# A hybrid decoder layer on one core: an adding load, a fifth weight slot and an earlier block product

## The chip, the core and the metric

One core of a Trainium2 chip runs the whole layer in one launch. TensorE (PE) multiplies, VectorE (DVE) and ScalarE (ACT) prepare its operands and take its results, GpSimd (POOL) does small work and issues some DMAs, SyncE (SP) issues most DMAs. The engines have a queue each, run it in order, and meet at semaphores. The metric is device time in microseconds from the first to the last instruction and what lies around them, lower is better.

## What is computed

```python
def reference(x, ...):
    h = rmsnorm(x, norm_pre_mix)
    proj = h @ w_in                          # 512 x 1024 by 1024 x 4168
    y_a = hgrn2_mixer(...)                   # gated linear recurrence
    y_b = dsa_mixer(...)                     # indexer, top 128 keys, attention
    x = x + rmsnorm(concat(y_a, y_b) @ w_o, norm_post_mix)
    h = rmsnorm(x, norm_pre_ffn)
    ff = silu(h @ w_gate) * (h @ w_up)       # hidden size 2816
    ff = ff @ w_down
    return x + rmsnorm(ff, norm_post_ffn)
```

Sequence 512, model width 1024, float32. The change touches the feed-forward part alone (the two lines that make `ff`, and the norm behind them).

## The kernel before

**Arithmetic.** Every weight matrix stays float32 in value: an operand is split into a high part, rounded to the type that the matmul takes, made by ACT, and a low part, the rest, made by DVE as operand minus high part. Each product is then three matmuls, low times high, high times low, high times high.

**Gate and up.** The first four chunks of 256 columns of the gate and up weights (`J_FF` to `J_FF + 3`) go through `feature_group` (L1638), 24 matmuls for each half `m` of a chunk. The other 18 (`NS`) go through a scheme that computes a 2 x 2 block product from seven smaller products: `block_product(n, i)` (L1978), 12 matmuls of 256 columns each. Product 1 of block `n` is passed on by ACT (`pass_on(n, 0)`, L960) to the bank in which product 6 accumulates, so product 6 waits for that copy. DVE makes the weight sums (`block_sums`, L1457 to L1461) and takes the results (`cut`, `take`, L1480 to L1495).

**Down.** `w_down` has 22 row tiles, in 11 pairs. They run in 21 steps `d` (`STEPS`): ten steps of kind "one" (pairs 0 to 9, the first sweep), one step "all" (pair 10, step `MID` = 10), ten steps "two" (pairs 0 to 9 again, the second sweep). A step "one" is four products of 6 matmuls of 512 columns (`step_product`, L2016), a step "two" three. Before a step, this happens:
- SP loads its weights into a raw slot (L599 to L604): for "one" two transfers, the whole first row tile (512 KB, columns 0 to 1023 of the slot) and the right half of the second row tile (256 KB, columns 1024 to 1535). There are four slots, `WL[d % 4]`, so the load of step `d` waits until PE has done step `d - 4`.
- DVE makes sums in place (`step_sums`, L1511 to L1513 for "one"). With the slot's four quarters q0 to q3: q2 = q2 + q1, then q1 = q0 + q1, then q3 = q2 + q0. For "two" two smaller sums (L1516, L1517).
- ACT sets one quarter aside for the second sweep (L971), makes the high parts of the weights (L979, `columns_of_step_hi`) and of the activations (L991 to L998).
- DVE makes the low parts of the weights (L1522, `columns_of_step_lo`) and of the activations (L1530 to L1536, `rows_of_step_lo`).

DVE's order in the first sweep is, for each `d`: `rows_of_step_lo(d)`, `step_sums(d + 1)`, `columns_of_step_lo(d)`. So the low weights of step `d` stand behind the arrival of the weights of step `d + 1`. In the second sweep it is `step_sums(d + 1)`, `columns_of_step_lo(d)`, `rows_of_step_lo(d)`. At the seam between block products and first sweep DVE runs `step_sums(1)`, `columns_of_step_lo(0)`, `take(16)`, and PE's step 0 waits for all three (`s_dlo`, `s_free`). PE runs steps 18, 19 and 20 in an interleaved order at the end: 18 matmuls of steps 18 and 19, then step 20 is wanted.

POOL issues, after the 36th block result (`s_gu2`), the load of the last gain, then waits for the end of the first sweep and reloads `x2`.

Of the kernel before, what the change touches and what calls it, by code (L numbers as in the profile page):

```python
# [7 lines left out]
P = 128  # L8
# [26 lines left out]
def hymba_layer(nc, x, w_in, lb_logits, hgrn_gnorm, rel_bias, w_o, norm_pre_mix, norm_post_mix,  # L35
# [3 lines left out]
    TB = S // P  # L39
# [70 lines left out]
    with ExitStack() as ctx:  # L110
# [3 lines left out]
        def sem(name):  # L114
            return ctx.enter_context(nc.semaphore(name))
# [53 lines left out]
        def a1(o, n):  # L169
            return A1[:, o:o + n]  # L170
# [44 lines left out]
        T_RAW = {1: a1(20480, 1024), 2: a1(21504, 1024), 3: a1(2048, 1024), 4: A2[:, 6912:7936]}  # L215
        RING = (0, 1, 4)
        SUMS = (3, 2)
        squares, fin = hT_f[:, 0:4 * D], hT_f[:, 4 * D:8 * D].rearrange("p (t n) -> p t n", t=TB)
        first_sum, third_sum = hT_f[:, 6144:7168], hT_f[:, 7168:8192]
        junk = a1(18432, 1024)  # L220
        junk_mid = a1(10240, 1024)
# [228 lines left out]

        WL = (0, 3, 2, 4)

        def step_raw(d):
            return W_f[:, WL[d % 4], :]

        def step_lo(d):
            return W_r[:, WL[d % 4], :]

        def step_hi(d):
            return (s_w[:, 0:CH], W_r[:, 1, :], s_t[:, 0:2, :].rearrange("p i n -> p (i n)"))[d % 3]  # L460
# [23 lines left out]
            return t.rearrange("p (k n) -> p k n", n=256)  # L484

        def down_landed(eng, d):
            eng.wait_ge(s_dw[d % 4], sum(32 if STEPS[e][0] == "one" else 16 for e in range(d % 4, d + 1, 4)))

        def steps_done(eng, n):
            if n == NB:  # L490
                eng.wait_ge(s_acc, 4)
            else:
                eng.wait_ge(s_step, n - (n > NB))
# [67 lines left out]
        @block.sync  # L561
        def _(sp):
            for t in range(TB):
                if t == 2:
                    sp.dma_start(raw_view(0)[:, 0:4, :], raw_src(0)[:, 0:4, :]).then_inc(s_raw_half, 16)
                sp.dma_start(xin[:, t, :], x_d[t * P:(t + 1) * P, :]).then_inc(s_x[t], 16)
            sp.dma_start(raw_view(0)[:, 4:8, :], raw_src(0)[:, 4:8, :]).then_inc(s_raw[0], 16)
            sp.dma_start(lbt[:, :, :], lb_logits.rearrange("r (h p) -> p r h", p=P)).then_inc(s_small, 16)
            sp.dma_start(gn[:, :], hgrn_gnorm.rearrange("a p -> p a")).then_inc(s_small, 16)
            sp.dma_start(tab, rel_bias).then_inc(s_small, 16)  # L570
            sp.dma_start(oh_sb, onehot).then_inc(s_small, 16)
            sp.dma_start(far[:, :], rel_bias[N_BUCKETS - 1, :].partition_broadcast(P)).then_inc(s_far, 16)
            for j in range(1, J_FF + 4):
                if j == J_IKW:
                    sp.dma_start(raw_view(j), raw_src(j)).then_inc(s_ikw, 16)
                    continue
                if ring_of(j) >= 2:
                    sp.wait_ge(s_lo, j - 2 if j - 2 <= J_IKW else j - 1)
                sp.dma_start(raw_view(j), raw_src(j)).then_inc(s_raw[ring_of(j) % 2], 16)
            for n, j in enumerate(range(J_FF + 4, J_DN)):  # L580
                if n < 2:
                    sp.wait_ge(s_lo, j - 1)
                elif n == 2:
                    sp.wait_ge(s_gu, 8)
                else:
                    sp.wait_ge(s_gu2, 2 * (n - 2))
                sp.dma_start(view(ring3(n), j), raw_src(j)).then_inc(s_raw3[n % 3], 16)
            for d, (kind, c) in enumerate(STEPS):
                if d == 0:
                    sp.wait_ge(s_gu2, 2 * (NS - 2))  # L590
                elif d < 3:
                    sp.wait_ge(s_prod, 3 * (NS - 2 + d))
                elif d == 3:
                    sp.wait_ge(s_gu2, 2 * NS)
                else:
                    steps_done(sp, d - 3)
                x, y = [wd[(2 * c + k) * P:(2 * c + k + 1) * P, :] for k in range(2)]
                if kind == "one":
                    sp.dma_start(step_raw(d)[:, 0:D], x).then_inc(s_dw[d % 4], 16)  # L599
                    sp.dma_start(step_raw(d)[:, D:D + 512], y[:, 512:D]).then_inc(s_dw[d % 4], 16)  # L600
                elif kind == "two":
                    sp.dma_start(step_raw(d)[:, 0:D], y).then_inc(s_dw[d % 4], 16)
                else:
                    sp.dma_start(view(step_raw(d), J_DN + c), raw_src(J_DN + c)).then_inc(s_dw[d % 4], 16)  # L604
            for i, t in enumerate(LAST):
                for half in range(2):
                    c = slice(half * 512, (half + 1) * 512)
                    sp.wait_ge(s_fin, 2 * i + half + 1)
                    sp.dma_start(out_d[t * P:(t + 1) * P, c], x2[:, t, c]).then_inc(s_out, 16)
            sp.wait_ge(s_out, 16 * 2 * TB)  # L610
# [3 lines left out]
        def _(pool):  # L614
# [99 lines left out]
                inv_of(8 + k)  # L714
            pool.wait_ge(s_x2, TB)
            pool.dma_start(x2_d, A2[:, 0:TB * D]).then_inc(s_x2s, 16)
            pool.wait_ge(s_gu2, 2 * NS)
            pool.dma_start(gain_out, norm_post_ffn[0, :].partition_broadcast(P)).then_inc(s_go, 16)
            pool.wait_ge(s_x2s, 16)
            steps_done(pool, NB)  # L720
# [365 lines left out]
        def _(dve):  # L1086
            n_chain = [0]

            def link(ins):
                n_chain[0] += 1  # L1090
                ins.then_inc(s_dve, 1)
                dve.wait_ge(s_dve, n_chain[0])
# [413 lines left out]
            def step_sums(d):  # L1506
                kind, c = STEPS[d]
                down_landed(dve, d)
                q = step_raw(d).rearrange("p (q n) -> p q n", q=4)
                if kind == "one":  # L1510
                    link(dve.tensor_tensor(q[:, 2], q[:, 2], q[:, 1], ALU.add))  # L1511
                    dve.tensor_tensor(q[:, 1], q[:, 0], q[:, 1], ALU.add)  # L1512
                    dve.tensor_tensor(q[:, 3], q[:, 2], q[:, 0], ALU.add).then_inc(s_dsum, 1)  # L1513
                else:
                    p = pair_raw(c)
                    dve.tensor_tensor(pieces(q[:, 2]), kept(c), pieces(q[:, 0]), ALU.add)  # L1516
                    dve.tensor_tensor(p[:, 1], p[:, 1], p[:, 2], ALU.add).then_inc(s_dsum, 1)  # L1517
# [117 lines left out]
        def _(pe):  # L1635
# [314 lines left out]
            GATE_UP_BANKS = {J_FF: (0, 1), J_FF + 1: (2, 3), J_FF + 2: S_BANKS[0][1:], J_FF + 3: S_BANKS[1][1:]}  # L1950
            for j in range(J_FF, J_FF + 4):
                pe.wait_ge(s_lo, j + 1)
                for m in range(2):
                    if j == J_FF + 2:
                        pe.wait_ge(s_t4, 3)
                    elif j == J_FF + 3:
                        pe.wait_ge(s_fr, m + 1)
                    feature_group(w_split(j), m, P, GATE_UP_BANKS[j][m], S // 2 if j < J_FF + 2 else 0, S, s_gu)

            def block_product(n, i, fresh=False):  # L1960
                y, z, f = S_BANKS[n % 2]
                out = {1: PS[:, y, 0:256], 2: PS[:, y, 0:256], 3: PS[:, z, 0:256], 4: PS[:, f, 0:256],
# [16 lines left out]
                                      stop=(k == 3 and p == 2), skip_group_check=True)  # L1979
                return o  # L1980

            pe.wait_ge(s_tlo, 3)
            for n in range(NS):
                pe.wait_ge(s_wl[0], n + 1)
                if n >= 2 and n % 2 == 0:
                    pe.wait_ge(s_free, n // 2)
                elif n >= 2:
                    pe.wait_ge(s_fr, n + 2)
                block_product(n, 1, True).then_inc(s_prod, 1)
# [123 lines left out]
```

## Time and profile before

| what | us |
|---|---|
| median of 3 runs (lowest, highest) | 667.36 (665.61, 667.52) |
| the profiled execution | 664.93 |
| its span, first to last instruction | 663.2 |
| PE busy in the span | 651.1 |
| DVE busy | 548.3 |
| ACT busy | 350.3 |
| POOL busy | 92.2 |
| first down sweep, first matmul of step 0 to that of step 10 | 543.91 to 603.36 |
| second down sweep, first matmul of step 11 to the last matmul | 614.24 to 657.01 |

The profile is of one execution, which was 2.4 us faster than the median of the timed runs. Times inside it are from the start of the span. PE is nearly always busy, so the first thing to look for is where it is not, and then who ends each of those gaps.

### The profile page before, as it was taken

How to read it: one execution, taken by the hardware profiler on the slowest of the kernel's cores; microseconds unless marked ns; L12 is line 12 of the kernel's file. 1: busy time of each engine (PE TensorE's matmuls, PEld its weight loads, DVE VectorE, ACT ScalarE, POOL GpSimd, SP SyncE). 2: the span in 40 equal slices, each digit the busy share in tenths (PEclk: the TensorE clock that was granted, in tenths of full speed). 3: DMA queues.
4: the chain of work that ended last, by engine and by line, in shares of the span. 5: the costliest groups of instructions: out<-in, count | busy, mean ns of one | idle time of the engine just before them, and what ended most of it. 6: DMA issues, size and time to landing. Idle time of an engine off the chain costs nothing.

```text
span 663.2 us, 10196 instructions
## 1 busy us (share of the span) xinstructions
PE 651.1 (98%) x4017; PEld 580.3 (88%) x4017; DVE 548.3 (83%) x769; ACT 350.3 (53%) x564; POOL 92.2 (14%) x131
## 2 busy tenths in 40 slices
PE   8999999999999999999999999999999999999986
PEld 6878888888888889888998999999999998778875
DVE  6766999998988768345886988989989979998787
ACT  6656433443349577235643555555554565663563
POOL 4800220000405378002100000000000000000001
PEclk9999999999999999999999999999999999999998
DMA  8453042352521301252332423324324235444423
GB/s 277 129 162 113 13 127 65 99 174 77 190 65 64 126 2 36 92 191 64 118 137 63 127 65 127 110 84 127 96 96 128 86 114 183 142 143 191 127 95 128
DMA packets 51266, 75.53 MB, mean 114 GB/s; under 512 B 5393, under 2 KB 40209, under 8 KB 50962
## 3 DMA queue, kind: packets, MB, share of 16 engines
q1 hardware_dynamic: 47360, 62.78, 29.8%
q0 software_dynamic: 3568, 11.55, 4.7%
q8 instruction: 32, 0.52, 0.3%
q10 hardware_dynamic: 290, 0.55, 0.2%
q14 instruction: 16, 0.13, 0.1%
HBM read 70.12 MB, written 6.84 MB: 116 GB/s over the span
## 4 chain that ended last, share of the span: by engine, by line
PE 86%; DVE 10%; ACT 2%; DMA 1%; issue 1%; POOL 0%; DVEq 0%; ACTq 0%; POOLq 0%
PE PS L1638 38%; PE PS L1978 27%; PE PS L2016 7%; PE PS L1857 2%; DVE W_r L1522 2%; PE PS L1712 2%; PE PS L2027 2%; PE PS L1688 1%; PE PS L1687 1%; PE PS L1868 1%; PE PS L1791 1%; PE PS L1682 1%; DVE W_f L1512 1%; DVE A L1630 1%; DVE W_f L1511 1%
## 5 line engine op out<-in xcount | busy, mean ns | idle before, releaser
L1638 PE MATMUL PS<-hT_lo,w_hi 128*128 128x512 f32 (+2 forms) x280 | 102.0, 364 | 0.0
L1638 PE MATMUL PS<-hT_hi,w_hi 128*128 128x512 f32 (+2 forms) x280 | 100.7, 360 | 0.0
L1638 PE MATMUL PS<-hT_hi,w_lo 128*128 128x512 f32 (+2 forms) x280 | 100.7, 359 | 0.0
L1097 DVE TENSOR_TENSOR w_lo<-raw,w_hi 128x2048 fp32r<-128x2048 f32 x21 | 48.1, 2291 | 18.9 <-ACT w_hi L732 18.8
L1978 PE MATMUL PS<-hT_hi,W_r 128*128 128x256 f32 x216 | 61.1, 283 | 0.0
L1978 PE MATMUL PS<-hT_hi,s_w 128*128 128x256 f32 x216 | 61.1, 283 | 0.0
L1978 PE MATMUL PS<-hT_lo,s_w 128*128 128x256 f32 x216 | 61.1, 283 | 0.0
L1638 PEld LDWEIGHTS PS<-hT_hi,w_hi 128*128 128x128 f32 (+1 forms) x280 | 52.5, 188 | 8.5
L1638 PEld LDWEIGHTS PS<-hT_lo,w_hi 128*128 128x128 f32 (+1 forms) x280 | 52.6, 188 | 7.4 <-issue 0.2
L1638 PEld LDWEIGHTS PS<-hT_hi,w_lo 128*128 128x128 f32 (+1 forms) x280 | 52.6, 188 | 7.1
L1978 PE MATMUL PS<-s_t,s_w 128*128 128x256 f32 x288 | 57.8, 283 | 0.6 <-ACT PS L960 0.6
L1978 PEld LDWEIGHTS PS<-s_t,s_w 128*128 128x128 f32 x288 | 47.5, 192 | 0.8 <-issue 0.8
L732 ACT ACTIVATE w_hi<-raw 128x2048 fp32r<-128x2048 f32 x21 | 40.1, 1912 | 14.7 <-PE PS L1638 14.0
L1468 DVE TENSOR_TENSOR W_r<-W_f,s_w 128x1024 fp32r<-128x1024 f32 x36 | 44.0, 1223 | 1.2 <-ACT s_w L945 0.2
L960 ACT ACTIVATE PS<-PS 128x256 f32<-128x256 f32 x54 | 19.9, 368 | 47.3 <-PE PS L1978 45.6
L1638 PE MATMUL PS<-w_lo,hT_hi 128*128 128x512 f32 x112 | 44.6, 398 | 0.0
L1638 PE MATMUL PS<-w_hi,hT_hi 128*128 128x512 f32 x112 | 43.7, 390 | 0.0
L1638 PE MATMUL PS<-w_hi,hT_lo 128*128 128x512 f32 x112 | 43.6, 389 | 0.0
L1978 PEld LDWEIGHTS PS<-hT_lo,s_w 128*128 128x128 f32 x216 | 41.5, 192 | 0.0
L1978 PEld LDWEIGHTS PS<-hT_hi,W_r 128*128 128x128 f32 x216 | 41.5, 192 | 0.0
L1978 PEld LDWEIGHTS PS<-hT_hi,s_w 128*128 128x128 f32 x216 | 41.5, 192 | 0.0
L1978 PE MATMUL PS<-s_t,W_r 128*128 128x256 f32 x144 | 40.7, 283 | 0.0
(293 smaller groups left out, 1701.2 us busy)
## 6 DMA issues: line engine op xcount, KB each, us to landing
raw<-in_w_in_dram SPq DMA_DIRECT2D x15, 1024.0 KB, 5.5
W_f<-in_w_down_dram SPq DMA_DIRECT2D x20, 512.0 KB, 3.5
W_f<-in_w_gate_dram SPq DMA_DIRECT2D x9, 1024.0 KB, 5.3
W_f<-in_w_up_dram SPq DMA_DIRECT2D x9, 1024.0 KB, 5.2
raw<-in_w_o_dram SPq DMA_DIRECT2D x4, 1024.0 KB, 5.0
W_f<-in_w_down_dram SPq DMA_DIRECT2D x10, 256.0 KB, 3.8
A<-in_x_dram SPq DMA_DIRECT2D x4, 512.0 KB, 5.6
A<-in_x_dram POOLq DMA_DIRECT2D x4, 512.0 KB, 5.4
```

The source lines that it names most:

```text
L732: act.activation(w_split(j)[0], raw_view(j), ACT.Copy).then_inc(s_hi, 1)
L960: act.activation(to, of, ACT.Copy, scale=scale).then_inc(s_seed, 1)
L1097: dve.tensor_tensor(lo, raw_view(j), hi.bitcast(F32), ALU.subtract).then_inc(s_lo, 1)
L1468: dve.tensor_tensor(block_lo(n)[:, :, c], block_raw(n)[:, :, c], block_hi(n)[:, :, c].bitcast(F32), ALU.subtract).then_inc(s_wl[2 if i els ...
L1511: link(dve.tensor_tensor(q[:, 2], q[:, 2], q[:, 1], ALU.add))
L1522: dve.tensor_tensor(step_lo(d)[:, 0:n], step_raw(d)[:, 0:n], step_hi(d)[:, 0:n].bitcast(F32), ALU.subtract).then_inc(s_dlo, 1)
L1638: o = pe.matmul(out, lhs[a], rhs[b], start=(first and n == 0), stop=(last and n == 2))
L1712: o = pe.matmul(PS[:, level_bank(l, p), h * P:(h + 1) * P], a, late(l)[:, m * P:(m + 1) * P], start=True, stop=True)
L1857: o = pe.matmul(PS[:, 4 + b % 2, h * DH:(h + 1) * DH], PT[u % 2][:, s * P:(s + 1) * P], av[:, s * W + h * DH:s * W + (h + 1) * DH], start= ...
L1978: o = pe.matmul(out, (hi, lo)[a][:, k, :], xs[b][:, k, :], start=(fresh and k == 0 and p == 0), stop=(k == 3 and p == 2), skip_group_check ...
L2016: o = pe.matmul(PS[:, bank + 2 * t, :], (hi, lo)[a][:, t * P:(t + 1) * P], w[b], start=(start and p == 0), stop=(p == 2), skip_group_check ...
L2027: o = pe.matmul(PS[:, 2 * t + half, :], x[a][:, k, t * P:(t + 1) * P], w[b][:, k, half * 512:(half + 1) * 512], start=False, stop=(p == 2) ...
```

## The change

1. Down, first sweep: q2 = q2 + q1 is no longer made by DVE. POOL waits until both transfers of step `d` have landed and issues a third one from memory, of the right half of the first row tile (128 x 512, 256 KB), which adds to what stands in the slot (`accum_op=ALU.add`). DVE makes q1 and then waits for this DMA before q3. POOL's loop over the ten steps stands ahead of the load of the last gain and of the `x2` reload.
2. Down, second sweep: from step 11 on the raw slots are five, the fifth being columns 2048 to 4095 of `hT_f`, whose contents nobody reads any more. The load of a step waits for the step that had the same slot, step 11's for none. `squares`, which used the same memory, moves to `A1`.
3. Gate and up: PE issues product 1 of block 0 between the two halves of chunk `J_FF + 3`, with its ACT copy following it, and no longer behind the second half.

```diff
-        squares, fin = hT_f[:, 0:4 * D], hT_f[:, 4 * D:8 * D].rearrange("p (t n) -> p t n", t=TB)
+        squares, fin = a1(0, 4 * D), hT_f[:, 4 * D:8 * D].rearrange("p (t n) -> p t n", t=TB)
...
+        def slot(d):
+            return d % 4 if d <= MID else (4, *((MID + i) % 4 for i in range(1, 5)))[(d - MID - 1) % 5]
+
+        def slot_before(d):
+            return max((e for e in range(d) if slot(e) == slot(d)), default=None)
+
         def step_raw(d):
-            return W_f[:, WL[d % 4], :]
+            return W_f[:, WL[slot(d)], :] if slot(d) < 4 else hT_f[:, CH:2 * CH]
...
-                else:
-                    steps_done(sp, d - 3)
+                elif slot_before(d) is not None:
+                    steps_done(sp, slot_before(d) + 1)
...
-            pool.wait_ge(s_gu2, 2 * NS)
+            for d in range(NB):
+                c = STEPS[d][1]
+                down_landed(pool, d)
+                pool.dma_start(step_raw(d)[:, D:D + 512], wd[2 * c * P:(2 * c + 1) * P, 512:D],
+                               accum_op=ALU.add).then_inc(s_dadd[d % 4], 16)
             pool.dma_start(gain_out, norm_post_ffn[0, :].partition_broadcast(P)).then_inc(s_go, 16)
...
                 if kind == "one":
-                    link(dve.tensor_tensor(q[:, 2], q[:, 2], q[:, 1], ALU.add))
-                    dve.tensor_tensor(q[:, 1], q[:, 0], q[:, 1], ALU.add)
+                    link(dve.tensor_tensor(q[:, 1], q[:, 0], q[:, 1], ALU.add))
+                    dve.wait_ge(s_dadd[d % 4], 16 * (d // 4 + 1))
                     dve.tensor_tensor(q[:, 3], q[:, 2], q[:, 0], ALU.add).then_inc(s_dsum, 1)
...
+                    elif j == J_FF + 3:
+                        if m == 1:
+                            pe.wait_ge(s_wl[0], 1)
+                            block_product(0, 1, True).then_inc(s_prod, 1)
+                        pe.wait_ge(s_fr, m + 1)
+                    feature_group(w_split(j), m, P, GATE_UP_BANKS[j][m], S // 2 if j < J_FF + 2 else 0, S, s_gu)
```

DVE around the sums of step 3 in the first sweep. Before:

```order
L1530 TENSOR_TENSOR A_r<-A,s_t 128x512 [waits ff_hi_ready]
L1531 TENSOR_TENSOR s_t<-A,s_t 128x512
L1511 TENSOR_TENSOR W_f<-W_f 128x512 [waits down_raw_landed3]
L1512 TENSOR_TENSOR W_f<-W_f 128x512 [waits dve_chain]
L1513 TENSOR_TENSOR W_f<-W_f 128x512
L1522 TENSOR_TENSOR W_r<-W_f,s_t 128x2048 [waits down_hi_ready]
```

And now:

```order
L1541 TENSOR_TENSOR A_r<-A,s_t 128x512 [waits ff_hi_ready]
L1542 TENSOR_TENSOR s_t<-A,s_t 128x512
L1522 TENSOR_TENSOR W_f<-W_f 128x512 [waits down_raw_landed3]
L1524 TENSOR_TENSOR W_f<-W_f 128x512 [waits down_first_sum_landed3,dve_chain]
L1533 TENSOR_TENSOR W_r<-W_f,s_t 128x2048 [waits down_hi_ready]
```

One sum is gone, and the last sum, with the low weights of step 2 behind it (the last row), now waits for POOL's DMA.

POOL from the set-aside of `x2` to its reload. Before:

```order
L716 DMA x_aside<-A 128x4096 [waits x2_ready]
L718 DMA A<-in_norm_post_ffn_dram 128x1024 [waits block_results]
L721 DMA A<-x_aside 128x4096 [waits first_sweep_products,x2_set_aside]
```

And now (ten adding loads, of which the first two stand here):

```order
L723 DMA x_aside<-A 128x4096 [waits x2_ready]
L727 DMA W_f<-in_w_down_dram 128x512 [waits down_raw_landed0]
L727 DMA W_f<-in_w_down_dram 128x512 [waits down_raw_landed1]
...
L729 DMA A<-in_norm_post_ffn_dram 128x1024
L732 DMA A<-x_aside 128x4096 [waits first_sweep_products,x2_set_aside]
```

The adding loads are added, and the gain's load has moved behind them.

PE in the last gate and up chunk. Before, its last matmuls (L1638), the first product of block 0 (reading `hT_lo` and `hT_hi`), then product 6 (reading `s_t`):

```order
L1638 MATMUL PS<-hT_hi,w_hi 128x512
L1978 MATMUL PS<-hT_lo,s_w 128x256
L1978 MATMUL PS<-hT_hi,W_r 128x256
L1978 MATMUL PS<-hT_hi,s_w 128x256
...
L1978 MATMUL PS<-s_t,s_w 128x256
```

And now:

```order
L1649 MATMUL PS<-hT_hi,w_hi 128x512
L1979 MATMUL PS<-hT_lo,s_w 128x256
L1979 MATMUL PS<-hT_hi,W_r 128x256
L1979 MATMUL PS<-hT_hi,s_w 128x256
...
L1649 MATMUL PS<-hT_lo,w_hi 128x512
...
L1649 MATMUL PS<-hT_hi,w_hi 128x512
L1979 MATMUL PS<-s_t,s_w 128x256
```

24 matmuls of the chunk's second half now stand between product 1 and product 6.

## Rows read from the trace of the kernel before

**Rows 1.** The page, second view: granted TensorE clock in 40 slices, in tenths.
```profile
PEclk9999999999999999999999999999999999999998
```

**Rows 2.** Waits of PE from 330 us on: waited for, us in total, times, longest.
```profile
PE PS L2016 <- DVE ff_lo L1533: 1.9, 1, 1.9
PE PS L2016 <- DVE W_r L1522: 0.9, 2, 0.5
PE PS L1978 <- ACT PS L960: 0.6, 1, 0.6
```

**Rows 3.** The chain of waits near the end: start, us, engine, what.
```profile
638.91 3.59 DMA W_f<-in_w_down_dram
...
643.55 1.67 DVE W_r L1522
645.22 0.88 DVE ff_lo L1533
```

**Rows 4.** Timeline of PE, first block product: start, us, [idle before <-releaser].
```profile
365.67 0.28 PE L1978 MATMUL PS<-hT_hi,s_w 128*128 128x256 f32 x1
366.56 0.36 PE L1978 MATMUL PS<-s_t,s_w 128*128 128x256 f32 x1 [0.61 <-ACT PS L960]
```

**Rows 5.** Timeline of ACT at the same place.
```profile
367.14 1.49 ACT L949 ACTIVATE s_w<-W_f 128x1536 fp32r<-128x1536 f32 x1 [0.73 <-DVE W_f L1459]
368.53 0.37 ACT L960 ACTIVATE PS<-PS 128x256 f32<-128x256 f32 x1
```

**Rows 6.** Timeline of PE in the down sweeps: first matmuls of steps, and the last gap.
```profile
543.91 0.47 PE L2016 MATMUL PS<-W_r,ah 128*128 128x512 f32 x1
...
545.62 0.35 PE L1978 MATMUL PS<-A_r,s_w 128*128 128x256 f32 x1
...
552.72 0.39 PE L2016 MATMUL PS<-W_r 128*128 128x512 f32 x1
...
558.16 0.40 PE L2016 MATMUL PS<-W_r,s_t 128*128 128x512 f32 x1
...
575.11 0.50 PE L2016 MATMUL PS<-W_r,s_t 128*128 128x512 f32 x1 [0.38 <-DVE W_r L1522]
...
586.85 0.50 PE L2016 MATMUL PS<-W_r 128*128 128x512 f32 x1 [0.51 <-DVE W_r L1522]
...
643.93 0.39 PE L2016 MATMUL PS<-s_w,ah 128*128 128x512 f32 x1
...
646.24 0.47 PE L2016 MATMUL PS<-W_r 128*128 128x512 f32 x1 [1.91 <-DVE ff_lo L1533]
```

**Rows 7.** Timeline of DVE at the seam: last sum of step 1, low weights, first of take(16).
```profile
539.55 0.68 DVE L1513 TENSOR_TENSOR W_f<-W_f 128x512 f32<-128x512 f32 x1
540.15 2.29 DVE L1522 TENSOR_TENSOR W_r<-W_f,s_w 128x2048 fp32r<-128x2048 f32 x1
542.36 0.68 DVE L1488 TENSOR_TENSOR A<-PS,A 128x512 f32<-128x512 f32 x1
```

**Rows 8.** Timeline of SP: second transfer of step 1, first transfer of step 3.
```profile
534.22 0.43 SPq L600 DMA_DIRECT2D W_f<-in_w_down_dram  x1
...
548.75 0.33 SPq L599 DMA_DIRECT2D W_f<-in_w_down_dram  x1
```

**Rows 9.** DMA issues: queue, count, KB each, median us from issue to landing.
```profile
W_f<-in_w_down_dram SPq DMA_DIRECT2D x10, 256.0 KB, 3.8
A<-in_x_dram POOLq DMA_DIRECT2D x4, 512.0 KB, 5.4
...
A<-bias_by_distance POOLq DMA_DIRECT2D x8, 128.0 KB, 2.4
...
A<-in_norm_post_ffn_dram POOLq DMA_DIRECT2D x1, 512.0 KB, 5.2
```

**Rows 10.** Timeline of ACT at the end: high parts of steps 19 (activations) and 20.
```profile
640.79 0.83 ACT L995 ACTIVATE W_r<-A 128x768 fp32r<-128x768 f32 x1
...
643.58 1.49 ACT L979 ACTIVATE s_t<-W_f 128x1536 fp32r<-128x1536 f32 x1 [0.34 <-DVE A L1517]
```

More of the change, by code:

```diff
@@ L330, in hymba_layer @@
         s_row = sem("ff_row_sums_ready")
-        s_dw = [sem(f"down_raw_landed{i}") for i in range(4)]
+        s_dw = [sem(f"down_raw_landed{i}") for i in range(5)]
         s_dsum = sem("down_sums_ready")
+        s_dadd = [sem(f"down_first_sum_landed{i}") for i in range(4)]
         s_dhi = sem("down_hi_ready")
@@ L451, in hymba_layer @@
         WL = (0, 3, 2, 4)
+        def slot(d):
+            return d % 4 if d <= MID else (4, *((MID + i) % 4 for i in range(1, 5)))[(d - MID - 1) % 5]
+        def slot_before(d):
+            return max((e for e in range(d) if slot(e) == slot(d)), default=None)
         def step_raw(d):
-            return W_f[:, WL[d % 4], :]
+            return W_f[:, WL[slot(d)], :] if slot(d) < 4 else hT_f[:, CH:2 * CH]
         def step_lo(d):
-            return W_r[:, WL[d % 4], :]
+            return W_r[:, WL[slot(d)], :] if slot(d) < 4 else hT_hi[:, :, :].rearrange("p k t -> p (k t)")[:, CH:2 * CH]
         def step_hi(d):
@@ L486, in down_landed @@
         def down_landed(eng, d):
-            eng.wait_ge(s_dw[d % 4], sum(32 if STEPS[e][0] == "one" else 16 for e in range(d % 4, d + 1, 4)))
+            eng.wait_ge(s_dw[slot(d)], sum(32 if STEPS[e][0] == "one" else 16 for e in range(d + 1) if slot(e) == slot(d)))
         def steps_done(eng, n):
@@ L594, in _ @@
                     sp.wait_ge(s_gu2, 2 * NS)
-                else:
-                    steps_done(sp, d - 3)
+                elif slot_before(d) is not None:
+                    steps_done(sp, slot_before(d) + 1)
                 x, y = [wd[(2 * c + k) * P:(2 * c + k + 1) * P, :] for k in range(2)]
                 if kind == "one":
-                    sp.dma_start(step_raw(d)[:, 0:D], x).then_inc(s_dw[d % 4], 16)
-                    sp.dma_start(step_raw(d)[:, D:D + 512], y[:, 512:D]).then_inc(s_dw[d % 4], 16)
+                    sp.dma_start(step_raw(d)[:, 0:D], x).then_inc(s_dw[slot(d)], 16)
+                    sp.dma_start(step_raw(d)[:, D:D + 512], y[:, 512:D]).then_inc(s_dw[slot(d)], 16)
                 elif kind == "two":
-                    sp.dma_start(step_raw(d)[:, 0:D], y).then_inc(s_dw[d % 4], 16)
+                    sp.dma_start(step_raw(d)[:, 0:D], y).then_inc(s_dw[slot(d)], 16)
                 else:
-                    sp.dma_start(view(step_raw(d), J_DN + c), raw_src(J_DN + c)).then_inc(s_dw[d % 4], 16)
+                    sp.dma_start(view(step_raw(d), J_DN + c), raw_src(J_DN + c)).then_inc(s_dw[slot(d)], 16)
             for i, t in enumerate(LAST):
@@ L1949, in _ @@
             pe.wait_ge(s_hlo, 2 * TB)
[L1950 to L1958, printed above, removed]
             def block_product(n, i, fresh=False):
@@ L1980, in block_product @@
                 return o
+            GATE_UP_BANKS = {J_FF: (0, 1), J_FF + 1: (2, 3), J_FF + 2: S_BANKS[0][1:], J_FF + 3: S_BANKS[1][1:]}
+            for j in range(J_FF, J_FF + 4):
+                pe.wait_ge(s_lo, j + 1)
+                for m in range(2):
+                    if j == J_FF + 2:
+                        pe.wait_ge(s_t4, 3)
+                    elif j == J_FF + 3:
[4 more added lines that the diff above has]
+                    feature_group(w_split(j), m, P, GATE_UP_BANKS[j][m], S // 2 if j < J_FF + 2 else 0, S, s_gu)
             pe.wait_ge(s_tlo, 3)
             for n in range(NS):
[L1984 to L1989, printed above, removed]
-                if n:
+                if n:
+                    pe.wait_ge(s_wl[0], n + 1)
+                    if n >= 2 and n % 2 == 0:
+                        pe.wait_ge(s_free, n // 2)
+                    elif n >= 2:
+                        pe.wait_ge(s_fr, n + 2)
+                    block_product(n, 1, True).then_inc(s_prod, 1)
                     pe.wait_ge(s_wl[2], n)
```

## The prediction

> **What bounds the kernel now.** The page's slices first: the granted clock is at the upper of its two levels (2.4 GHz) all along [rows 1], so the clock is no term. By the page's busy times (the table above) PE works 651.1 of 663.2 us, so only PE's gaps can be gained. The list of waits from 330 us on names all of them: 1.9 us in one piece, 0.9 us in two, 0.6 us in one [rows 2]. Measured from the start that a matmul would have had at its usual distance from the one before (0.12 us for 256 columns; for 512 a step's (558.16 - 552.72)/24 = 0.227 us [rows 6]), to the start it had, these are:
> - 365.67 + 0.12 = 365.79, in fact 366.56: 0.8 us until ACT's copy behind the first block product [rows 4].
> - Step 5 of the first sweep 0.5 us late, step 7 0.7 us late, both for DVE's low weights [rows 6]. DVE then had an extra pair of row sums to make.
> - 643.93 + 0.23 = 644.16, in fact 646.24: 2.1 us in the last steps [rows 6]. The chain of waits tells why: the load of step 20 is issued at 638.91, when PE has left step 16's slot, lands 3.6 us later, and only behind its sums does DVE make the low parts of step 19 [rows 3].
>
> Together 4.1 us, 0.6% of the time: that is all the change can win here. The three edits aim at the three gaps.
>
> **Part 3, the earlier first product.** Nothing is added, 12 matmuls (1.4 us) change place with 24. ACT's copy then runs under the second half of the chunk and the 0.8 us go. But that half ends 1.4 us later relative to the block products, and DVE's product of it and the sums of block 1 stand behind it. PE reaches product 6 at 365.8, and DVE's sums for ACT are ready 1.4 us later than now. ACT's copy into high parts, now at 367.14, runs at 368.6, and the seed copy behind it, now at 368.53 [rows 5], at 370.0 to 370.4. PE wants that seed at 365.8 + 3 x 1.44 = 370.1 and gets it about 0.3 us late. Net gain 0.8 - 0.3 = 0.5, between 0 and 0.8; I take 0.4.
>
> **Part 2, the fifth slot.** Step 20's load is issued one step (18 x 0.227 = 4.1 us) sooner, so DVE isn't held. What is late next: ACT makes step 19's high activations at 640.79 for 0.83 us [rows 10], and DVE's low parts (1.67 + 0.88 us [rows 3]) end at about 643.5, before 644.16: the 2.1 us gap closes. Step 20 then is wanted at 644.16 + 12 x 0.227 = 646.9. Its high weights wait for step 17's end and for two squares, so they start at about 643.4 instead of 643.58 [rows 10], the high activations end at 645.6, the low parts at 647.4: PE waits 0.5. Net gain 2.1 - 0.5 = 1.6, between 1.2 and 2.1. Loads of steps 11 to 19 also come sooner, where PE has no gap to win.
>
> **Part 1, the adding load.** Removed: ten sums of DVE, 0.6 to 0.7 us each (the last sum of a step advances DVE by 540.15 - 539.55 = 0.6 [rows 7]). While PE isn't waiting for DVE that wins nothing, at steps 5 and 7 it wins the 0.5 + 0.7 = 1.2 us. Added: ten POOL DMAs of 256 KB and a wait for each, and the wait is the trouble. It stands in DVE's queue ahead of the low weights of the step before, and the DMA can't be issued before the two plain transfers have landed, so two transfers now stand one behind the other. Call X the time from POOL's issue to landing. No row shows an adding DMA. The bounds: a 128 KB load of POOL lands in 2.4 us, a 512 KB one in 5.2 and 5.4 with others beside it [rows 9]. The adding load brings 256 KB, and must also read and rewrite 256 KB in place, so 512 KB are touched; and SP's next load starts while it runs. I take X = 4.2, a little nearer to the upper rows, and keep 2.4 and 5.4.
> - *Seam.* Step 1's second transfer is issued at 534.22 [rows 8], lands 3.9 later at 538.1; POOL wakes 0.1 later and its DMA lands at 538.2 + X. Behind that: last sum 0.6 + 0.1, low weights 2.2 (542.36 - 540.15), `take(16)` 1.4 (two operations like that at 542.36) [rows 7], 0.1 to PE: step 0 can start at 542.7 + X = 546.9 against 543.91 [rows 6], 2.9 late (X - 1.3). The cover that hides it today is the time from landing to use, and it is 1.3 us. The 0.2 us that PE waits before 545.62 [rows 6] go, which leaves 2.7.
> - *Step 2.* The load of step 3 is issued when PE has done the last block product, 548.75 [rows 8] + 2.6 = 551.35. From there to step 2's low weights: 0.4 to the second issue, 3.8 to its landing [rows 9], 0.1, X, 0.1, sum 0.6, low weights 2.2, 0.1: 7.3 + X. Step 2 starts at 551.35 + 11.5 = 562.85 against 558.16 [rows 6]: 4.7 late.
> - *Steps 3 to 9.* A step takes PE 558.16 - 552.72 = 5.45 us. The load of step d + 1 is issued at the end of step d - 3, 5.45 + 0.2 after that one's start, so step d can't start before 12.95 + X after step d - 3; PE itself needs 3 x 5.45 = 16.35. Above X = 3.4 every third step falls behind, by 0.8 at 4.2: steps 5 and 8, 1.6 in all. From that comes off the 1.2 that steps 5 and 7 wait today. End of the sweep: 4.7 + 1.6 - 1.2 = 5.1 late.
> - The gain's load, now behind the tenth adding load, is wanted only after 648 us; the `x2` reload waits for the sweep's end as now. Free.
>
> Here a rule of the Trainium skill speaks against the edit: DMA: Bandwidth & Descriptors, Rules for kernel authors, says to issue a DMA early and wait on it late, so that its fixed cost overlaps. Here it can't: the adding DMA has to be issued on the landing of another. The same page (Anatomy of one DMA, SWDGE path) gives a POOL DMA 2.0 us plus its bytes at 436 GB/s; by that, an estimate, X would be 2.6. The 128 KB row agrees with it, the 512 KB rows are 2 us above.
>
> **Sum.** 5.1 - 1.6 - 0.4 = +3.1 us. On the profiled execution 664.93 + 3.1 = 668.0; that one lies 2.4 below the median of the runs, and I forecast the median: 667.36 + 3.1 = **670.5 us**.
>
> **Rivals.**
> - *A, a short adding load.* If adding costs the DMA engines nothing that shows, X = 2.8 (128 KB row plus a little). Seam 1.5 late, 1.3 after the small wait; step 2 starts at 548.75 + 1.3 + 7.3 + 2.8 = 560.15, 2.0 late; no step falls behind (15.75 under 16.35), the 1.2 come off: 0.8. Then 0.8 - 2.0 = -1.2, 666.2 us, no change. At X = 2.4 it is 0 - 2.0, 665.4. For it: the 128 KB row; against it: each POOL load of 512 KB took over 5. It decides below X = 3.4. The page's fit above belongs to this case.
> - *B, a long adding load.* X = 5.2, as the gain's 512 KB at this very place. Seam 3.9 late; step 2 at 548.75 + 3.7 + 12.5 = 564.95, 6.8 late; steps 5 and 8 1.8 each, less 1.2: 9.2. Less 2.0 is +7.2, 674.6 us. Beyond it, each us of X costs 4 (seam, step 2, steps 5 and 8).
> - *C, a part doesn't do what it says.* The end gap may stay, if step 20's or 19's high parts hold PE instead: the 1.6 don't come, 672.1 us. Against it: the times in part 2 leave 0.7 us for step 19.
>
> **Numbers.** About what a measurement of this kernel can tell from no change is 0.3%, 2 us: 665.4 to 669.4 is "same". Forecast band, X from 3.4 to 4.8: 0.47, of which 0.14 (X up to 3.9) lies within 2 us of before. A 0.27, of which 0.06 is faster by over 0.3%. B 0.22. C 0.04. So faster 0.06, same 0.21 + 0.14 = 0.35, slower 0.33 + 0.22 + 0.04 = 0.59. The range goes from A's cheap end to past B: 665.6 (X just above 2.4) to 676.0 (X = 5.5); 0.2 is left out, a little below, most above, where adding costs more than any row here.
>
> **What would show it.** Right: POOL's ten DMAs landing 3.5 to 4.8 us after issue; DVE waiting for them before the last sum of most steps; step 0's first matmul 2 to 4 us after the last of the 17th block's product 5; gaps of PE before step 2, 5 and 8; no wait of DVE for DMA in the second sweep and a gap before steps 19 and 20 under 0.8 us together; PE going from product 1 of block 0 to the chunk's second half and on with at most 0.4 us lost. Wrong: X under 3.4, with no gap at steps 5 and 8 (A); X over 5 (B); or SP's own loads much slower than 3.8 us beside the adding ones, which my sum leaves as they are.

## The result, and the profile after

| | before | after |
|---|---|---|
| median of 3 runs (lowest, highest), us | 667.36 (665.61, 667.52) | 679.71 (679.65, 680.63) |
| profiled execution, its span, us | 664.93, 663.2 | 679.65, 677.9 |
| PE busy, us | 651.1 | 655.8 |
| first sweep, first matmul of step 0 to that of step 10 | 543.91 to 603.36 | 548.47 to 619.70 |

The changed kernel is slower: ratio 1.020, interval 1.0168 to 1.0227. The forecast was 670.5 us with a range up to 676.0. The direction was right, the size was not: +12.4 us on the medians, +14.7 us on the two spans, where +3.1 was worked out.

The page of the changed kernel, busy time of the engines, and the granted clock in 40 slices (the one of before is [rows 1]):

```profile
PE 655.8 (97%) x4017; PEld 584.3 (86%) x4017; DVE 542.1 (80%) x759; ACT 350.0 (52%) x564; POOL 101.5 (15%) x141
...
PEclk9999999999999999999999999999999988989998
```

DVE works 6 us less, as the ten removed sums let one expect, and the time rose all the same. Slices 33, 34 and 36, which lie in the first down sweep, show a clock below full, which before had none. PE itself is "busy" 4.7 us longer with the same products to make: it ran some of them slower.

The list of PE's waits from 330 us on, against [rows 2]:

```profile
PE PS L2030 <- DVE W_r L1533: 8.4, 3, 4.9
PE PS L2030 <- DVE A L1501: 4.4, 1, 4.4
PE PS L2030 <- DVE ff_lo L1544: 0.3, 1, 0.3
```

ACT's copy (0.6 before) is gone from it. The wait for DVE's low activations (1.9 before) has shrunk to 0.3, before step 20; a second 0.3, at the seed of a block product, shows only in the spacing (370.51 to 370.91). And 12.8 us in four pieces stand where there were 0.9 in two. The same on PE's timeline (start, us, what, [idle before <-releaser]), to be read against [rows 4] and [rows 6]:

```profile
366.09 0.39 PE L1649 MATMUL PS<-hT_hi,w_hi 128*128 128x512 f32 x1
366.31 0.28 PE L1979 MATMUL PS<-s_t,s_w 128*128 128x256 f32 x1
...
548.47 0.76 PE L2030 MATMUL PS<-W_r,ah 128*128 128x512 f32 x1 [4.38 <-DVE A L1501]
...
568.87 0.79 PE L2030 MATMUL PS<-W_r,s_t 128*128 128x512 f32 x1 [4.89 <-DVE W_r L1533]
...
575.94 0.39 PE L2030 MATMUL PS<-W_r,ah 128*128 128x512 f32 x1
...
587.88 0.50 PE L2030 MATMUL PS<-W_r,s_t 128*128 128x512 f32 x1 [0.84 <-DVE W_r L1533]
...
596.28 0.79 PE L2030 MATMUL PS<-W_r,ah 128*128 128x512 f32 x1 [2.67 <-DVE W_r L1533]
...
619.70 0.39 PE L2041 MATMUL PS<-W_r 128*128 128x512 f32 x1
...
663.70 0.47 PE L2030 MATMUL PS<-W_r,s_t 128*128 128x512 f32 x1 [0.31 <-DVE ff_lo L1544]
...
671.75 0.39 PE L2030 MATMUL PS<-s_t 128*128 128x512 f32 x1
```

Step 0 waits (548.47), step 2 waits (568.87), steps 5 and 6 wait (587.88, 596.28). At its first matmul, step 0 is 4.6 us later than before, step 2 10.7, step 3 (575.94, before 563.64) 12.3, step 10 (619.70, before 603.36) 16.3, the last matmul (671.75, before 657.01) 14.7.

The chain of waits through the two largest gaps (start, us, what) shows what each is made of:

```profile
534.41 5.36 DMA W_f<-in_w_down_dram
...
540.05 3.95 DMA W_f<-in_w_down_dram
...
554.78 3.97 DMA W_f<-in_w_down_dram
558.75 0.28 issue
559.03 6.80 DMA W_f<-in_w_down_dram
...
565.92 0.69 DVE W_f L1524
566.61 2.21 DVE W_r L1533
```

Each is two transfers one behind the other: SP's second one of the step, then POOL's adding one. At the seam it is SP's that is slow (5.4 us, while the adding load of step 0, issued at 532.84, runs), at step 2 it is POOL's (6.8 us, while SP's two transfers of the next step, issued at 558.57 and 558.94, run). The DMA issues of the page (count, KB each, median us from issue to landing), where [rows 9] had 3.8 for the first of these:

```profile
W_f<-in_w_down_dram SPq DMA_DIRECT2D x10, 256.0 KB, 4.6
W_f<-in_w_down_dram POOLq DMA_DIRECT2D x10, 256.0 KB, 4.0
```

The median of 4.0 hides two groups: the ten adding loads, of steps 0 to 9, took 4.1, 4.0, 3.9, 6.8, 6.2, 4.0, 4.3, 5.9, 3.8 and 4.0 us. What tells the groups apart is when SP issues its pair for the next step. The three long ones (steps 3, 4 and 7) were issued within 0.5 us of it. Four of the others (steps 1, 2, 5 and 9) had nothing of SP's beside them, and three (steps 0, 6 and 8) had been under way for 1.1 to 1.4 us when the pair was issued. Those three were not slowed, but SP's second transfer then took 5.4, 5.0 and 5.6 us.

Then the clock. Stretches of the trace before, in and behind the slow parts (from and to, length, busy times of PE, PEld, DVE, ACT and POOL, granted clock, DMA share, GB/s; all times in us):

```profile
540.00:548.10 8.10, 4.08 (x35) 3.88 (x33) 4.52 (x5) 5.21 (x10) 0.87 (x1) 1.00 0.50 129
548.17:551.58 3.41, 3.12 (x8) 2.57 (x9) 3.38 (x4) 1.46 (x3) 0.86 (x1) 0.50 0.42 64
551.60:560.00 8.40, 8.40 (x49) 7.36 (x49) 5.42 (x9) 2.86 (x3) 0.86 (x1) 1.00 0.40 104
568.65:572.06 3.41, 3.19 (x8) 2.52 (x9) 3.38 (x6) 2.15 (x5) 0.86 (x1) 0.50 0.26 66
...
595.95:599.36 3.41, 3.08 (x7) 2.48 (x8) 3.34 (x7) 1.57 (x3) 0.00 (x0) 0.50 0.54 187
```

Toward the end of each of the three long gaps the granted clock falls from 1.00 to 0.50, from 2.4 to 1.2 GHz, and stays there for 3.4 us. Step 2 then takes 575.94 - 568.87 = 7.07 us instead of 5.45: 1.6 us more, in a place where PE waits for nobody.

### The profile page after: what moved, and what is told of

Read it like the earlier page. It is cut to its first block, busy times and chain, and to the rows that moved or that the text cites. A ratio compares the mean times of both kernels' runs of the same rounds, so it can differ in the third digit from the quotient of the medians.

```text
span 677.9 us, 10205 instructions
## 1 busy us (share of the span) xinstructions
PE 655.8 (97%) x4017; PEld 584.3 (86%) x4017; DVE 542.1 (80%) x759; ACT 350.0 (52%) x564; POOL 101.5 (15%) x141
## 4 chain that ended last, share of the span: by engine, by line
PE 87%; DMA 5%; DVE 5%; ACT 2%; issue 1%; POOL 0%; SPq 0%; DVEq 0%; ACTq 0%
PE PS L1649 37%; PE PS L1979 25%; PE PS L2030 10%; DMA W_f<-in_w_down_dram 5%; PE PS L1868 2%; PE PS L1723 2%; PE PS L2041 2%; PE PS L1699 1%; PE PS L1698 1%; PE PS L1879 1%; DVE W_r L1533 1%; PE PS L1802 1%; PE PS L1693 1%; DVE A L1641 1%; PE PS L1793 1%
## 5 line engine op out<-in xcount | busy, mean ns | idle before, releaser
L727 POOL DMA_DIRECT2D W_f<-in_w_down_dram x10 | 8.6, 865 | 266.5 <-DMA W_f<-in_w_down_dram 266.5
```

Of the source, the lines that this page charges most:

```text
L727: pool.dma_start(step_raw(d)[:, D:D + 512], wd[2 * c * P:(2 * c + 1) * P, 512:D], accum_op=ALU.add).then_inc(s_dadd[d % 4], 16)
```

## The experiments

All ran beside the kernel before, whose median was 666.67 us beside the first four runs, 665.81 beside the next four and 666.90 beside the last two. Ratios are to those.

### Without the adding load, and with it alone

`e1_no_adding_load` is the changed kernel with DVE's first sum back and POOL's loop gone; parts 2 and 3 stay.

```diff
-            for d in range(NB):
-                c = STEPS[d][1]
-                down_landed(pool, d)
-                pool.dma_start(step_raw(d)[:, D:D + 512], wd[2 * c * P:(2 * c + 1) * P, 512:D],
-                               accum_op=ALU.add).then_inc(s_dadd[d % 4], 16)
+            pool.wait_ge(s_gu2, 2 * NS)
...
-                    link(dve.tensor_tensor(q[:, 1], q[:, 0], q[:, 1], ALU.add))
-                    dve.wait_ge(s_dadd[d % 4], 16 * (d // 4 + 1))
+                    link(dve.tensor_tensor(q[:, 2], q[:, 2], q[:, 1], ALU.add))
+                    dve.tensor_tensor(q[:, 1], q[:, 0], q[:, 1], ALU.add)
```

> The changed kernel with its first part undone: DVE makes the sum q2 + q1 again, POOL has no adding loads and waits for the block results before the gain's load. Five slots and the earlier product stay. Theory P (the adding load alone makes the loss, the other two parts win what their gaps hold): the gap behind the first block product stays closed (0.4 to 0.5 us net), the gap at steps 19 and 20 is 0.5 us where it was 2.1, the first sweep is as before (two gaps, 0.5 and 0.7 us); a span 2.1 us under before's, 661.1 us, ratio 0.997. Rival Q (the five slots or the early loads also hurt, for instance by traffic): the first sweep has gaps or loads that before hasn't, and the span is at or over 663.

Measured: 663.30 us, ratio 0.9944 (0.9929 to 0.9959). Faster than before. Its list of PE's waits has the two of steps 5 and 7 from before, and the end:

```profile
PE PS L2026 <- DVE W_r L1529: 0.9, 2, 0.5
PE PS L2026 <- DVE ff_lo L1540: 0.3, 1, 0.3
```

`e2_adding_load_alone` is the kernel before with that same piece put in, and nothing else.

> The kernel before with the first part alone: ten adding loads of POOL, DVE's first sum removed, DVE's wait. Theory P: the loss of the first sweep is this part's alone, the sweep ends 16 to 17 us later than before and nothing is won back at the end, 680 to 682 us, ratio 1.025. Rival Q (the three parts together do it): clearly under 677 us, ratio under 1.015.

Measured: 684.08 us, ratio 1.0253 (1.0230 to 1.0275). The last matmul ends 17.3 us later than before. PE's waits:

```profile
PE PS L2021 <- DVE W_r L1527: 7.3, 3, 4.1
PE PS L2021 <- DVE A L1495: 3.8, 1, 3.8
PE PS L2021 <- DVE ff_lo L1538: 1.8, 1, 1.8
```

It follows that part 1 is the whole loss: 679.7 - 663.3 = 16.4 us by the first of the two, 684.1 - 666.7 = 17.4 by the second. The other two parts win 666.7 - 663.3 = 3.4 us on the medians. In the gaps the two profiles show 2.1 of it, 1.6 at the end and 0.5 at the first product (their spans differ by 1.8). The rest is not assigned: the runs of the kernel before lie between 665.4 and 669.3 us, those of e1 between 663.0 and 663.9, so one of the gaps that e1 closes may be longer in other executions than in the one profiled.

### What of the adding load costs: the second transfer, or the adding

`e3_plain_for_adding` is the changed kernel with plain POOL loads. They write the quarter q2 over instead of adding to it, so q2 lacks one of its two terms; waits, order and bytes from memory are those of the changed kernel.

```diff
-                pool.dma_start(step_raw(d)[:, D:D + 512], wd[2 * c * P:(2 * c + 1) * P, 512:D],
-                               accum_op=ALU.add).then_inc(s_dadd[d % 4], 16)
+                pool.dma_start(step_raw(d)[:, D:D + 512], wd[2 * c * P:(2 * c + 1) * P, 512:D]
+                               ).then_inc(s_dadd[d % 4], 16)
```

> The changed kernel with POOL's ten loads plain instead of adding; same bytes from memory, same place, same waits. The sum q2 therefore lacks one term, the output is not the reference's. Theory M (meeting transfers are the price: POOL's load runs behind or among SP's next one): the plain load takes nearly as long as the adding one, median over 3.5 us and 5 to 7 us where SP issues beside it, and the time stays above 673 us. Rival N (adding itself is the price): the plain load lands in about 2.7 us, and the time falls to 668 or under.

Measured: 669.85 us, ratio 1.0051 (1.0036 to 1.0065), 9.9 us less than the changed kernel, which lies between what the two theories gave. The ten POOL loads took 2.7, 2.7, 2.8, 4.3, 3.8, 2.7, 2.8, 4.2, 4.0 and 2.8 us: adding costs 1.1 to 1.5 us more where SP's pair is not issued at the same time, and 1.7 to 2.5 us more where it is (4.3 against 6.8, 3.8 against 6.2, 4.2 against 5.9). The gaps stay, by the spacing 2.3 us at the seam, 2.3 before step 2 and 2.0 before step 6:

```profile
546.07 0.47 PE L2030 MATMUL PS<-W_r,ah 128*128 128x512 f32 x1 [2.12 <-DVE A L1501]
563.88 0.50 PE L2030 MATMUL PS<-W_r,s_t 128*128 128x512 f32 x1 [2.18 <-DVE W_r L1533]
587.83 0.50 PE L2030 MATMUL PS<-W_r,ah 128*128 128x512 f32 x1 [1.82 <-DVE W_r L1533]
```

POOL's DMA queue on the three pages (packets, MB, share of 16 engines), first of the kernel before, then of this one, then of the changed kernel:

```profile
q0 software_dynamic: 3568, 11.55, 4.7%
```

```profile
q0 software_dynamic: 4368, 14.17, 5.9%
```

```profile
q0 software_dynamic: 5008, 14.17, 7.0%
```

Ten plain loads add 800 packets, ten adding ones 1440, for the same 2.6 MB: 80 against 144 for a load. The Trainium skill (Collectives: The Full Stack, Part 3, on why ReduceScatter is half of AllGather) says that an add in the DMA path needs two source reads and two descriptors for each piece, one of them for the operand that stands at the place. That page has no time for a load like this one. The counts go the same way without showing it: by the sizes in the trace a plain load is 64 packets of 4 KB and 16 of 4 bytes, an adding one 128 of 2 KB and 16 of 4 bytes. Both carry the same 256 KB, so no second read shows as bytes. What does show is that an adding packet of 2 KB took 178 ns in the median, a plain one of 4 KB 159 ns, so the packets of an adding load kept the DMA engines busy for twice as long. Whether the second read or the finer split is behind that, no run separates.

So two causes hold. Serial landing alone, with a plain second transfer, makes the kernel 3.2 us slower than before in place of 3.4 faster (e1), so it costs 6.6 us; one stretch of slow clock, at the seam, is in that. The adding costs the other 9.9. It doubles the gaps at the seam and at step 2 (4.5 for 2.3 and 5.1 for 2.3), makes the one at step 6 2.8 instead of 2.0 and adds one of 1.0 at step 5, and two more stretches of slow clock come with them. The changed kernel and e3 were timed beside different runs of the kernel before (667.36 and 666.67), so this division is good to some 0.7 us.

### The clock

`e4_pe_kept_busy` is the changed kernel with matmuls of zeros by a constant matrix (128 columns each) that PE runs while it would wait, 18 products ahead of step 0, 20 ahead of step 2, 10 ahead of step 6. They add zero to the output. POOL makes the zeros long before, ahead of its loop.

```diff
             def step_ready(d):
+                for n in range({0: 18, 2: 20, 6: 10}.get(d, 0)):
+                    pe.matmul(PS[:, 0, 0:P], mirror[:, :], M0[:, :], start=(d == 0), stop=True,
+                              skip_group_check=True)
                 pe.wait_ge(s_dlo, d + 1)
```

> The changed kernel with matmuls of zero by a constant put on PE ahead of its waits at steps 0, 2 and 6 of the first sweep (18, 20 and 10 of 128 columns, about 0.22 us each), which add zero to a bank. Theory C (three stretches of 3.4 us at half clock behind the three long gaps cost 1.5 us each): no such stretch in the first sweep, span 3 to 5 us under 677.9, 673 to 675. Rival D (the halved clock falls on time that PE would wait anyway): stretches gone, but the span within 1 us of 677.9, since step 3's and step 7's loads set the pace.

Measured: 675.59 us, ratio 1.0126 (1.0103 to 1.0148), 4.1 us less than the changed kernel. Clock slices of its page, then PE around step 0 and step 2 (L2050 are the zeros, with two records for each product):

```profile
PEclk9999999999999999999999999999999999999999
```

```profile
544.16 4.18 PE L2050 MATMUL PS<-M,mirror 128*128 128x128 f32 x36
549.15 0.47 PE L2032 MATMUL PS<-W_r,ah 128*128 128x512 f32 x1 [0.81 <-DVE A L1503]
...
563.08 4.63 PE L2050 MATMUL PS<-M,mirror 128*128 128x128 f32 x40
567.46 0.48 PE L2032 MATMUL PS<-W_r,s_t 128*128 128x512 f32 x1
```

Nothing that DVE or the DMAs do was changed, step 0 starts even 0.7 us later than in the changed kernel, and the span is 4.0 us shorter. The three slow stretches are gone, and with them most of what each had cost, by the step times 1.4 to 1.6 us: from step 0's first matmul to step 1's it takes 8.5 us instead of 9.9.

### From which step, and how many slots

The forecast put most of the loss at the seam and at step 2. `e5_adding_from_step_4` leaves steps 0 to 3 to DVE.

```diff
-            for d in range(NB):
+            for d in range(4, NB):
...
+                    if d < 4:
+                        link(dve.tensor_tensor(q[:, 2], q[:, 2], q[:, 1], ALU.add))
...
-                    dve.wait_ge(s_dadd[d % 4], 16 * (d // 4 + 1))
+                    if d >= 4:
+                        dve.wait_ge(s_dadd[d % 4], 16 * (d // 4 + 1 - 4 // 4))
```

> The changed kernel with adding loads for steps 4 to 9 alone; in steps 0 to 3 DVE makes the sum. Theory S (the chain landing, POOL, adding load, low weights is too long everywhere in the sweep): steps 0 to 2 start as in the kernel before (543.9, 552.7, 558.2), step 3 about 2.7 us late, and more gaps at every third step behind it; adding loads take 4 us alone, about 6 beside SP's; sweep's end 4 to 10 us late, span 666 to 672. Rival T (only the seam and step 2, where loads come last, cost; later the slots are ahead): no gaps behind step 2, DVE's relief closes the two gaps at steps 5 and 7, span 660 us.

Measured: 673.44 us, ratio 1.0106 (1.0084 to 1.0128). The seam and step 2 are whole again, but the gaps come back further on, as theory S had it, though the first is at step 4 and not 3 (step 3 waits only 0.6 us). PE's timeline:

```profile
572.54 0.50 PE L2033 MATMUL PS<-W_r 128*128 128x512 f32 x1 [2.27 <-DVE W_r L1536]
591.23 0.50 PE L2033 MATMUL PS<-W_r 128*128 128x512 f32 x1 [0.43 <-DVE W_r L1536]
599.89 0.51 PE L2033 MATMUL PS<-W_r,s_t 128*128 128x512 f32 x1 [2.92 <-DVE W_r L1536]
```

The chain ahead of the first of them (step 4) is step 5's second transfer and its adding load, 4.60 and 5.89 us:

```profile
558.72 4.60 DMA W_f<-in_w_down_dram
...
563.62 5.89 DMA W_f<-in_w_down_dram
```

Two of its gaps are again followed by 3.4 us of a granted clock of 0.50 (from 572.94 and from 600.25).

`e6_five_slots_adding_from_4` is e5 and gives the first sweep the fifth slot too, whose memory is free at that point: a step's load then waits for the step five before it.

```diff
         def slot(d):
-            return d % 4 if d <= MID else (4, *((MID + i) % 4 for i in range(1, 5)))[(d - MID - 1) % 5]
+            return d % 5
```

> As the run before this one, and five raw slots in the first sweep too (slot d mod 5 for all steps), so that each load from step 4 on is issued a step, 5.45 us, sooner. Theory S: 5.45 us more cover is enough for an adding load of 6 us; DVE waits for none, its relief closes the gaps of 0.5 and 0.6 us at steps 5 and 7, span 1.2 us under e1's 661.4, 660.2, ratio to before 0.992 to 0.993. Rival U (the adding loads' traffic slows SP's loads or DVE so that the gain is eaten): span at or over 661.4.

Measured: 662.23 us, ratio 0.9941 (0.9928 to 0.9953). The whole list of PE's waits from 330 us on:

```profile
PE PS L2033 <- DVE ff_lo L1547: 0.3, 1, 0.3
```

The transfers are no quicker. The chain at step 5 and DVE's wait for it:

```profile
553.50 5.72 DMA W_f<-in_w_down_dram
...
559.52 6.95 DMA W_f<-in_w_down_dram
```

```profile
566.55 0.69 DVE L1527 TENSOR_TENSOR W_f<-W_f 128x512 f32<-128x512 f32 x1 [1.18 <-DMA W_f<-in_w_down_dram]
```

The adding load took 6.95 us, longer than any in the changed kernel, and of this one only 1.2 us reached DVE and 0.2 us, by the spacing, PE. What spares PE is that the loads of step 5 were issued a step sooner (553.1 against 558.4 us in e5). e5 and e6 differ in the slots alone, and by 11.2 us.

`e7_five_slots_no_adding` is e1 with the fifth slot (`d % 5`), to see what the slot gives by itself.

> The kernel of e1 (no adding load, earlier product, five slots in the second sweep) with five slots in the first sweep too. Theory: the gaps at steps 5 and 7 come from DVE's own work, so earlier loads change nothing, span 661.4 within 0.3, both gaps as in e1; ratio to before 0.994 to 0.997. Rival (they come from late loads): gaps gone, 660.2.

Measured: 663.35 us, ratio 0.9966 (0.9954 to 0.9978). The waits of steps 5 and 7 are there as in e1 (0.55 and 0.62 us): they come from DVE's work, not from loads. One new gap, 1.9 us before step 2, was not expected. The chain ahead of it begins with step 3's second transfer:

```profile
548.77 6.59 DMA W_f<-in_w_down_dram
...
555.38 0.70 DVE W_f L1518
```

and SP's queue shows the two transfers of step 4, into the new slot, right behind it:

```profile
549.25 0.43 SPq L606 DMA_DIRECT2D hT_f<-in_w_down_dram  x1
549.72 0.46 SPq L607 DMA_DIRECT2D hT_f<-in_w_down_dram  x1
```

Two steps' loads together made the first one take 6.6 us instead of some 4. It isn't in each execution: e6 has the same four issues and its step 3 came in time, and five of the seven timed runs of e7 lie at 663.2 to 663.5, the profiled one at 664.9 and another at 664.6. That this transfer is what tells those apart is argued from one profile, not shown.

`e8_five_slots_adding_all` is the changed kernel, adding loads from step 0 on, with five slots.

> The changed kernel with five slots in both sweeps and adding loads in all ten steps. Theory S: the seam (4.5 us) and step 2 (5.0 us) keep their gaps, since loads 0 to 3 come no sooner, with a stretch of half clock behind each (1.1 and 1.6 us); no gap at steps 5 and 6; sweep's end about 11 us late, span 671 to 673. Rival T (gaps later in the sweep stay): span 677 or more.

Measured: 674.89 us, ratio 1.0133 (1.0117 to 1.0149). As the theory had it, only the two gaps that a fifth slot can't cover are left (4.9 and 5.0 us by the spacing), and none behind them:

```profile
548.64 0.58 PE L2030 MATMUL PS<-W_r,ah 128*128 128x512 f32 x1 [4.74 <-DVE A L1501]
...
569.09 0.61 PE L2030 MATMUL PS<-W_r,s_t 128*128 128x512 f32 x1 [4.82 <-DVE W_r L1533]
```

Each is followed by 3.4 us at a granted clock of 0.50; step 10 is 11.2 us later than before.

### Is a hidden adding load worth anything

e1 and e6 had run beside different runs of the kernel before, so both ran once more on one chip: `e9_no_adding_again` is e1, `e10_five_adding_again` is e6.

> The kernel of e1_no_adding_load a second time, on the same chip as e10: four slots in the first sweep, DVE makes all sums. Both theories: 663 us, ratio 0.994 to 0.996, PE's gaps before steps 5 and 7 of 0.5 and 0.6 us as in the first.

> The kernel of e6_five_slots_adding_from_4 a second time, beside e9. Theory G (an adding load that is issued a step ahead is hidden, and takes the 1.1 us of gaps before steps 5 and 7 away): the two kernels differ by 0.6 to 1.2 us, this one 662 us, ratio 0.992 to 0.994, and no gap in the first sweep. Theory Z (what the adding loads save DVE comes back as slower steps and as slower loads beside them, so that they are worth nothing at all): the two medians within 0.4 us.

Measured: 663.29 us (662.92 to 663.85) and 662.09 us (661.91 to 662.19), ratios 0.9952 (0.9939 to 0.9964) and 0.9932 (0.9918 to 0.9945). The highest run of the second lies below the lowest of the first. The 1.2 us are the waits of steps 5 and 7 (0.54 + 0.66 in e9), which the removed sums take away. The two kernels differ in the fifth slot of the first sweep as well, but e7 has that slot without adding loads, keeps both waits, and lies 1.1 us above e6, which ran beside it. So the edit's purpose is sound and is worth 1.1 to 1.2 us, no more. e10's kernel, with adding loads from step 4 on and five slots in both sweeps, is the fastest of all that ran.

## Where the prediction was right, and where it failed

**What bounds the kernel: right. How much there is to win: a little low.** The gaps summed to 4.1 us, "all the change can win here". e10's profile shows 3.3 of them closed (0.5 is left at the end, 0.3 at the seed), and its span is 2.7 us shorter than that of before. By the medians it is 4.8 us below its kernel before, more than the gaps of one profile hold. Where the difference lies no profile shows.

**Part 3: right.** The 0.8 us before product 6 are gone (366.31 stands 0.22 behind 366.09), and PE waits 0.3 us for the seed copy at 370.9. Net 0.5 where 0.4 was put.

**Part 2: right to the tenth.** The lateness falls from 16.3 at step 10 to 14.7 at the last matmul: 1.6. PE's wait before step 20 is 0.5 by the spacing (663.00 + 0.23 to 663.70), as forecast.

**Part 1: mechanism and places right, size wrong by a factor of three** (16.4 for 5.1). The steps, as the prediction put them:

- *"I take X = 4.2"* as one number for all ten. For seven loads it was well placed: 3.8 to 4.3 us, in the four that ran alone and in the three that had a lead of over 1 us on SP's pair. What failed is that it is a constant. The text itself says that SP's next load starts while it runs, and then gives that no price of its own. Three loads were issued within 0.5 us of SP's pair and took 5.9 to 6.8 us, beyond the upper end of the bounds (5.4) too. At step 2 this is 2.6 us of the miss.
- *SP's own loads, "which my sum leaves as they are."* At the seam the second transfer of step 1 landed 5.4 us after its issue instead of 3.9, since the adding load of step 0 ran beside it. The other runs bear that out: this transfer took 4.9 to 5.8 us in the four kernels that have an adding load at step 0, 4.3 in e3 with a plain one, and 3.7 to 4.0 in the seven that have none. That is 1.5 of the 1.6 us by which step 0 started later than forecast (548.47 against 546.9). The rest of the seam's sum, from the landing to the first matmul, was 4.5 us forecast and 4.5 measured (544.00 to 548.47).
- *"So the clock is no term."* It was read off a kernel whose gaps are all 2.1 us or less, and taken over to one for which the same text forecast gaps of 3 and 5 us. Three of them brought 3.4 us at half clock each; e4 puts their price at 4.0 us in all. It also feeds on: the load of step 3 is issued when PE has done the last block product, which stands behind the first matmuls of step 0, so their slow clock (1.5 us) delays it by as much.
- *Step 2* was to start at 562.85 and did at 568.87. The 6.0 us are 1.5 from the seam's transfer, 1.5 from the clock behind it, 2.6 from X, and 0.4 in small terms, of which 0.2 is POOL, which woke 0.28 us after the landing and not 0.1. (The terms that the prediction lists there add up to 7.2 + X, not 7.3 + X; that is rounding.)
- *"By 0.8 at 4.2: steps 5 and 8, 1.6 in all."* The recurrence was right in kind, the places were steps 5 and 6. Step 7's loads (5.04 for the second transfer, 5.91 for the adding one) were both slow, so step 6 waited 2.8 us. With its slow clock the stretch from step 3 to 10 added 16.3 - 12.3 = 4.0 us where 0.4 was forecast.

Rival B (X = 5.2, 674.6 us) came nearer, though not by its mechanism: the mean X was 4.7, it left SP's loads as they were, and it left the clock at full. That e4, with the clock mended, came to 675.6 is in part luck. Rival A's short transfer is what e3 has, and even with it the kernel was slower than before (669.85): its forecast of 666.2 at 2.8 us failed on the same points, since loads issued together with SP's took 3.8 to 4.3, SP's transfer at the seam 4.3, and one gap brought a slow stretch.

The list of what would make the prediction wrong ended on "SP's own loads much slower than 3.8 us beside the adding ones". It named the risk, but neither the range nor the sum held a price for it. No row of before has such a transfer beside another one; the nearest, POOL's 512 KB at 5.2 and 5.4 us, would still have been short of the 5.9 to 6.8 us.

## What to carry to other kernels

A transfer that may start only when another has landed belongs a whole slot ahead of its use: adding loads from step 4 on gave 673.4 us with four slots and 662.2 with five, though they were no quicker, and there they won 1.2 us over none. Where the slot can't come sooner, at steps 0 to 3, the fifth did not help (e8). No run tried to put DVE's wait behind the low weights of the step before instead. Price a moved or added transfer twice, alone and beside whatever the other queues issue in that time. Ask which of them is issued first, and price those others again too. And when a sum gives a gap of PE that is longer than any in the profile at hand, ask that the clock be a term: here the three long gaps cost 4.0 us more than their length.

## What the runs showed of the hardware

- An adding load of 256 KB took 3.9 to 4.0 us alone (changed kernel), the plain one from the same queue 2.7 to 2.8 (e3), with 144 and 80 packets. Its instruction kept POOL 0.86 us instead of 0.54.
- Transfers that met slowed each other, but by the order of their issue. In the kernels with four slots (changed kernel, e2, e4, e5) every adding load that was issued within 0.5 us of SP's pair took 5.7 to 6.8 us, and one issued 0.65 us behind it 4.8 (e2); with a lead of 0.95 us or more on it, 3.8 to 4.3. Plain loads of POOL within 0.4 us of it took 3.8 to 4.3 (e3). SP's second transfer, of 256 KB, took 4.5 to 5.9 us beside an adding load in either case, instead of 3.8 to 4.0 (changed kernel). One of SP's with the next step's two right behind it on its own queue took 6.6 (e7) in one execution and 4.3 to 4.4 in two others (e6, e10).
- The granted clock fell to 0.50 for 3.4 us around the end of gaps of 2.3 us (e3, seam), 2.4 and 3.1 (e5), 2.7 (e2), 2.8, 4.5 and 5.1 (changed kernel), and 4.9 and 5.0 (e8). In e2 gaps of 4.0 and 4.3 us brought twice that, 6.8 us each. It didn't fall at gaps of 2.3 and 2.0 (e3, steps 2 and 6), of 1.9 (e7) and of 2.1 (the kernel before). Two gaps of 2.3 us in one execution went either way, so length alone doesn't decide there. What else does stays open.
